# The last expert quad's down weights packed in rows of one expert, with one set of products behind the third unit

## The chip, the cores and the metric

One of the cores of a Trainium2 chip runs the kernel. The metric is the device time of one execution in microseconds.

## The reference

Two transformer blocks for 256 tokens of width 1024 (272 with the meta tokens in the first mixer), all in float32. The first block is a mixer (a gated linear recurrence and an RG-LRU branch), then a routed mixture of experts. The second has dilated attention, spatial gating and a dense feed-forward. The change touches the mixture of experts. There are 32 experts, in 4 groups of 8; each token takes 2 experts of one group. Each expert computes

```
y = (silu(xb @ w_gate[e]) * (xb @ w_up[e])) @ w_down[e]
y * wts
```

with w_gate and w_up of 1024 x 512 and w_down of 512 x 1024. The results are added to the tokens with their routing weights, and a norm follows, with which the second block begins.

## The kernel before

The kernel is written for the engines by hand: each engine has its own program, and they meet at semaphores. The 32 experts are done in 8 quads of 4 experts. Each expert has room for 32 tokens (CAP), so a quad fills 128 rows. TensorE works on the four experts of a quad in four column groups of 32, which run side by side.

**Units and slots.** The weights of a quad are 24 MB. SP loads them as 12 units of 2 MB (j = 0 to 11): four of w_gate, four of w_up, four of w_down. Units lie in 12 slots of SBUF, in an order given by MOE_SLOTS; unit m waits until `unit_used` tells that the unit 12 before it is used. In most quads a unit is the whole matrix of one expert (`whole(q, j)`), 16 KB in a row on each partition. In the last quad the down units (j = 8 to 11) are split otherwise. w_down is viewed as (p k) n: partition p holds four rows k = 0 to 3 of 1024 floats, 4 KB each, which lie behind one another in memory. Units 8, 9 and 10 hold row k = 0, 1 and 2 of all four experts (`expert_unit`, one transfer each, four pieces of 4 KB on each partition). Unit 11 holds row k = 3 of all four in two transfers, columns 0 to 511 and then 512 to 1023, in pieces of 2 KB (L642 and L643; the second counts on a semaphore of its own, `last_landed`). `load` (L580) issues a transfer and lets it add 16 to the semaphore `landed<slot>`; `landed_values` (line 137) works out the values that `take_moe` (L1249) waits for on TensorE. Behind the experts' units SP issues, in the same queue, the units of block 2: first five or more of w_in_2 (2 MB each, pieces of 2 KB), each when its slot is free.

**TensorE in a quad.** `products_of_four` (L1199) multiplies the tokens with the four gate units, then with the four up units. ScalarE and VectorE make the hidden values of them; `turn_hidden` (L1205) and `turn_weights` (L1211) turn them, and ScalarE copies them to `hT` (L1981). In quads 1 to 6 `down_of_four` (L1237) waits for the four down units and does 32 matmuls. In the last quad `down` (L1227) is called for k = 0, 1, 2: it waits for unit 8 + k, does 8 matmuls (2 halves of 512 columns x 4 experts) into banks 2 and 3, and gives the unit back with `unit_used`. In the trace a float32 matmul has two records, so 8 matmuls are x16.

**The end of the stage.** `down_last(0)` (L1245) waits for unit 11's first transfer and finishes columns 0 to 511. ScalarE copies bank 2 (L2021), `combine((0,))` (L1218) adds the result to the tokens (four matmuls of 128 x 512), `down_last(1)` does the other half once `last_landed` is there. VectorE copies the sums (L2773), `turn_half(0)` (L1341) turns them, `combine((1,))` follows. Then `take2(0)` waits for w_in_2's first unit, and `steps` (L1353) begins its products. The second half is copied and turned behind the first of them; the norm's statistics are applied later. From there on block 2 runs.

**Slots.** Units 8, 9, 10 of the last quad lie in slots 8, 1 and 2. Slots 1 and 2 are taken next by w_in_2's fifth and sixth unit (B2_SLOTS), which wait for `unit_used` of 94 and 95.

Of the kernel before, what the change touches and what calls it, by code (L numbers as in the profile page):

```python
# [25 lines left out]
CAP = 32  # L26
QE = P // CAP
# [30 lines left out]
MOE_UNITS = QUADS * QUNITS  # L58
# [4 lines left out]
NSLOT = 12  # L63
MOE_SLOTS = [11, 5, 3, 6, 7, 4, 0, 9, 8, 1, 2, 10]
# [21 lines left out]
def whole(q, j):  # L86

    return not (q == 0 and j < 8) and not (q == QUADS - 1 and j >= 8)


def transfers(name, block):

    return 2 if (name == "lru" or (block == 2 and name.startswith("ff"))) else 1


def b1_slot(u):

    return u % RING1
# [39 lines left out]
def landed_values():  # L138


    total = [0] * NSLOT
    b1, moe, b2 = [], [], []
    for u, name in enumerate(B1_UNITS):
        total[b1_slot(u)] += 16 * transfers(name, 1)
        b1.append(total[b1_slot(u)])
    for m in range(MOE_UNITS):
        total[MOE_SLOTS[m % NSLOT]] += 32 if m == NSLOT - 1 else 16
        moe.append(total[MOE_SLOTS[m % NSLOT]])
    for n, name in enumerate(B2_UNITS):
        total[B2_SLOTS[n % RING]] += 16 * transfers(name, 2)  # L150
        b2.append(total[B2_SLOTS[n % RING]])
    return b1, moe, b2


LANDED1, LANDED_MOE, LANDED2 = landed_values()


# [116 lines left out]
def build(nc, A, out):  # L274
    ctx = ExitStack()
    with ctx:
# [5 lines left out]
        def S(name):  # L282
            if name not in sems:
                sems[name] = ctx.enter_context(nc.semaphore(name))
            return sems[name]

        bank = [ctx.enter_context(nc.psum_tensor(f"bank{b}", [P, 512], F32)) for b in range(8)]
# [21 lines left out]
        def slot(k):  # L309

            if k == NSLOT - 1:
                return extra[:, :]
            return ring[:, k, :] if k < RING else arena[:, WORK + (k - RING) * UW:WORK + (k - RING + 1) * UW]

        def w3(s, k):
            return slot(s).rearrange("p (k n) -> p k n", k=k)
# [82 lines left out]
        def bufs(o, ysb, sg):  # L399
            return Bufs(o[:, 0:D].rearrange("p (c n) -> p c n", c=KC), o[:, D:D + DE].rearrange("p (k n) -> p k n", k=4),  # L400
                        o[:, 1536:1792].rearrange("p (t e s) -> p t e s", t=NT, e=QE),
                        o[:, 1792:2048].rearrange("p (t e s) -> p t e s", t=NT, e=QE),
                        o[:, 2048:2304].rearrange("p (t n) -> p t n", t=NT), ysb, sg)

        hrow = h.rearrange("p t d -> p (t d)")
        main = bufs(arena, hrow[:, 0:D], hrow[:, D:D + DE])
# [168 lines left out]
        def _(sp):  # L575
# [3 lines left out]
            def load(s, src, dst):  # L579
                sp.dma_start(dst, src).then_inc(S(f"landed{s}"), 16)  # L580
# [10 lines left out]
            for u, name in enumerate(B1_UNITS):  # L591
                s = b1_slot(u)
# [24 lines left out]
            down_w = A["w_down"][0].rearrange("e (p k) n -> p e k n", k=4)  # L617

            def expert_unit(j, e):
                j4 = j % 4  # L620
                if j < 8:
                    return (gate_w, up_w)[j // 4][:, bass.ds(e, QE), 2 * j4:2 * j4 + 2, :]
                return down_w[:, bass.ds(e, QE), j4:j4 + 1, :]

            def expert_dst(s, j):
                return slot(s).rearrange("p (e k n) -> p e k n", e=QE, k=2 if j < 8 else 1)
# [6 lines left out]
            def load_unit(s, q, j):  # L633

                if whole(q, j):
                    w = (gate_w, up_w, down_w)[j // 4][:, QE * q + j % 4, :, :]
                    load(s, w, slot(s).rearrange("p (k n) -> p k n", k=KC if j < 8 else 4))
                elif j < 11:
                    load(s, expert_unit(j, QE * q), expert_dst(s, j))
                else:  # L640
                    w = slot(s).rearrange("p (e n) -> p e n", e=QE)
                    load(s, down_w[:, QE * q:QE * q + QE, 3, 0:512], w[:, :, 0:512])  # L642
                    sp.dma_start(w[:, :, 512:1024], down_w[:, QE * q:QE * q + QE, 3, 512:1024]) \  # L643
                        .then_inc(S("last_landed"), 16)

            for m in range(MOE_UNITS):
# [16 lines left out]
                s = MOE_SLOTS[m % NSLOT]  # L663
# [21 lines left out]
                if m == NSLOT - 1:  # L685
                    load_last_down(slice(3, 4))
                else:
                    load_unit(s, m // QUNITS, m % QUNITS)


            for n, name in enumerate(B2_UNITS):
                s = B2_SLOTS[n % RING]
# [17 lines left out]
                else:  # L710
                    c = 4 * int(name[2:])
                    m = min(4, FC - c)
# [84 lines left out]
        def _(pe):  # L797
            mm = nc.tensor.matmul
            tr = nc.tensor.transpose

            def take1(u):
                pe.wait_ge(S(f"landed{b1_slot(u)}"), LANDED1[u])
                return b1_slot(u)
# [70 lines left out]
            for t in range(NT):  # L874
# [4 lines left out]
                for k in range(KC):  # L879
# [9 lines left out]
                    last = mm(b[:, :], rT[:, k, t * P:(t + 1) * P], w3(0, KC)[:, k, :], start=(k == 0), stop=(k == KC - 1))  # L889
# [171 lines left out]
            def columns(first, m):  # L1061

                return bank[first + m % 4][:, (m // 4) * T:(m // 4 + 1) * T]
# [6 lines left out]
            for m in (2, 6, 3, 7, 1, 5, 0, 4):  # L1070
# [4 lines left out]
                for k in range(HEADS):  # L1075
                    last = mm(columns(4, m), w3(b1_slot(13), 4)[:, k, m * P:(m + 1) * P],  # L1076
                              oT[:, k, :], start=(k == 0 and m < 4), stop=(k == HEADS - 1), skip_group_check=True)
            last.then_inc(S("projected_a"), 1)
            unit_out(pe, NH - 1)
            for part in range(2):  # L1080
                s = take1(14 + part)
                pe.wait_ge(S("ob_ready"), part + 1)
                for m in range(KC):
                    if part and m >= 4:
                        pe.wait_ge(S("merged"), m - 3)
                    for k in range(4):
                        last = mm(columns(0, m), w3(s, 4)[:, k, m * P:(m + 1) * P], ly[:, 4 * part + k, :],  # L1087
                                  start=(part == 0 and k == 0 and m < 4), stop=(part == 1 and k == 3),
                                  skip_group_check=True)
# [73 lines left out]
            def expert(s, n):  # L1163

                w = slot(s).rearrange("p (e n) -> p e n", e=QE)
                return w if n == 4 else w.rearrange("p e (k n) -> p e k n", k=2)
# [55 lines left out]
            def down(k, s, o=main):  # L1222

                w = expert(s, 4)
                for half in range(2):
                    for e in range(QE):
                        last = mm(bank[2 + half][e * CAP:(e + 1) * CAP, :], o.hT[:, k, e * CAP:(e + 1) * CAP],  # L1227
                                  w[:, e, half * 512:(half + 1) * 512], start=(k == 0), stop=(k == 3))
                return last

            def down_of_four(slots):
# [6 lines left out]
                                      w[e][:, k, half * 512:(half + 1) * 512], start=(k == 0), stop=(k == 3))  # L1238
                return last

            def down_last(half, s):

                w = expert(s, 4)
                for e in range(QE):
                    last = mm(bank[2 + half][e * CAP:(e + 1) * CAP, :], main.hT[:, 3, e * CAP:(e + 1) * CAP],  # L1245
                              w[:, e, half * 512:(half + 1) * 512], start=False, stop=True)
                return last

            def take_moe(m):  # L1249
                pe.wait_ge(S(f"landed{MOE_SLOTS[m % NSLOT]}"), LANDED_MOE[m])  # L1250
                return MOE_SLOTS[m % NSLOT]
# [34 lines left out]
            for q in range(QUADS):  # L1286
                m = QUNITS * q
# [36 lines left out]
                    pe.wait_ge(S("xgT_rest"), q + 2)  # L1324
                if q + 1 < QUADS:
                    down_of_four([take_moe(m + 8 + e) for e in range(QE)]).then_inc(S("unit_used"), QE)
            for k in range(3):
                down(k, take_moe(m + 8 + k)).then_inc(S("unit_used"), 1)
            down_last(0, take_moe(m + 11)).then_inc(S("first_half"), 1)
            pe.wait_ge(S("weights_copied"), QUADS)  # L1330
            pe.wait_ge(S("y_first"), 1)
# [125 lines left out]
            for p in range(PAIRS):  # L1457
# [15 lines left out]
                if p == 0:  # L1473
                    pe.wait_ge(S("s_diag"), 2)
                    for t in range(NT):
                        last = mm(bank[7][:, t * P:(t + 1) * P], ones[:, :], s_diag[:, t, :], start=True, stop=True)
# [12 lines left out]
                if p == PAIRS - 1:  # L1489
                    pe.wait_ge(S("ws_masked"), 1)  # L1490
                    pe.wait_ge(S("qk_copied"), 12)
                    for g in range(SG):
                        last = tr(bank[6 + g // 4][:, (g % 4) * P:(g % 4 + 1) * P], wsr[:, g * P:(g + 1) * P],
                                  ident[:, :])
# [8 lines left out]
            for n in range(AH):  # L1503
                j, tile = n // 2, n % 2
# [14 lines left out]
                for hh in range(2):  # L1519
                    for b in range(4):  # L1520
                        last = tr(bank[2 + hh][:, b * P:(b + 1) * P], sc[n % 2][:, hh, b * P:(b + 1) * P], ident[:, :])
# [10 lines left out]
                for b, (g, kt) in enumerate(blocks):  # L1532
                    for hh in range(2):
                        hd = 2 * j + hh
                        last = mm(bank[4 + 2 * (n % 2)][hh * HD:(hh + 1) * HD, 0:P],
                                  vv[:, kt, g * 512 + hd * HD:g * 512 + (hd + 1) * HD],
                                  PTb[:, hh * 512 + b * P:hh * 512 + (b + 1) * P], start=(b == 0), stop=(b == 3))
# [4 lines left out]
            for t in range(NT):  # L1542
                for g in range(SG):
                    last = mm(bank[4 + t][:, g * HD:(g + 1) * HD], wsT[:, g, :],
                              uv[:, t, 512 + g * HD:512 + (g + 1) * HD], start=True, stop=True)
# [13 lines left out]
            for q, (src, lo) in enumerate(((aT, 0), (sT, 4))):  # L1559
# [3 lines left out]
                for m in range(KC):  # L1563
# [4 lines left out]
                    for k in range(4):  # L1568
                        last = mm(columns(lo, m), w3(su, 4)[:, k, m * P:(m + 1) * P], src[:, k, :],  # L1569
                                  start=(k == 0), stop=(k == 3))  # L1570
# [119 lines left out]
            for n in range(FD_LAST):  # L1690
# [6 lines left out]
                for i in (5, 6, 7):  # L1697
                    last = down_product(i, n)
# [5 lines left out]
            for i in (1, 6, 5, 2, 3, 7, 4):  # L1704
                for n in range(FD_LAST, FD_UNITS):
                    last = down_product(i, n)
# [1575 lines left out]
```

## Time and profile before

| what | value |
|---|---|
| median of 3 runs | 1191.41 us (1190.79 to 1191.93) |
| profiled execution | 1192.67 us, its span 1190.6 us |
| TensorE (PE) busy | 1021.0 us, 86% |
| VectorE (DVE) busy | 532.7 us, 45% |
| ScalarE (ACT) busy | 220.4 us, 19% |
| moved by DMA | 318.51 MB, mean 268 GB/s |
| chain that ended last | PE 66%, DMA 29%, DVE 2% |
| mean granted clock of TensorE | 0.938 |

The span runs from the first to the last instruction in the profile; the execution's time is a little longer. The chain that ended last is followed back from the last instruction, at each step to what released it. TensorE's granted clock is given as a share of 2.4 GHz: 1.00 is 2.4 GHz, 0.50 is 1.2 GHz, and a stretch with both shows a mean. In rows of a timeline the idle time before an instruction and what ended it stand in square brackets. PE is TensorE, PEld its weight loads, SPq SP's queue with its DMA issues. "arena", "ring", "extra" and "bank" are memories: the slots lie in the first three, the banks are those of PSUM.

### The profile page before, as it was taken

The numbers are of one execution on the slowest core, as the hardware profiler recorded it, in microseconds if no ns is written. First come the engines' busy times: TensorE is split into PE (matmuls) and PEld (weight loads), VectorE is DVE, ScalarE is ACT, GpSimd is POOL, SyncE is SP. The second block draws the span as 40 slices with busy tenths as digits, with TensorE's granted clock in tenths as the row PEclk, the third lists the DMA queues.
The fourth block names the chain that finished last, engine by engine and source line by source line (L and its number), as shares of the span: only waits on it lengthen the run. The fifth ranks groups of instructions, "written<-read, shape, count | busy, mean of one in ns | idle before, by whom it ended". The sixth has DMA issues, their size and how long they took to land.

```text
span 1190.6 us, 15216 instructions
## 1 busy us (share of the span) xinstructions
PE 1021.0 (86%) x6492; PEld 680.7 (57%) x6492; DVE 532.7 (45%) x919; ACT 220.4 (19%) x459; POOL 17.1 (1%) x53
## 2 busy tenths in 40 slices
PE   8999999999747474747474689999999999999997
PEld 4999999855222222212222234444799859999743
DVE  6758847672110101000100038755887866566634
ACT  2535355011000000000000022222333101111001
POOL 1000000000000000000000010000000000000000
PEclk9999999999887887887887899999999999999999
DMA  9642438998999999999999995555442426644400
GB/s 343 208 159 82 138 139 303 347 353 364 429 429 428 427 426 428 429 426 428 428 428 427 415 389 217 185 194 197 167 143 74 140 86 216 193 161 157 163 0 35
DMA packets 88542, 318.51 MB, mean 268 GB/s; under 512 B 8852, under 2 KB 34568, under 8 KB 77720
## 3 DMA queue, kind: packets, MB, share of 16 engines
q1 hardware_dynamic: 80560, 314.58, 67.7%
q10 hardware_dynamic: 7912, 2.92, 1.0%
q8 instruction: 53, 0.87, 0.3%
q14 instruction: 17, 0.14, 0.0%
HBM read 316.44 MB, written 1.05 MB: 267 GB/s over the span
## 4 chain that ended last, share of the span: by engine, by line
PE 66%; DMA 29%; DVE 2%; SPq 1%; ACT 1%; issue 1%; POOL 0%; POOLq 0%; DVEq 0%; ACTq 0%
DMA arena<-in_w_up 27%; PE bank L910 11%; PE bank L1602 11%; PE bank L1453 9%; PE bank L1685 6%; PE bank L1199 5%; PE bank L1386 4%; PE bank L1113 4%; DMA ring<-in_w_in 3%; PE bank L1569 2%; PE bank L1087 2%; PE bank L1190 1%; PE bank L1076 1%; PE bank L889 1%; PE bank L985 1%; PE bank L1443 1%
## 5 line engine op out<-in xcount | busy, mean ns | idle before, releaser
L1199 PE MATMUL bank<-arena 128*32 128x512 f32 x336 | 124.5, 724 | 51.1 <-DMA arena<-in_w_up 51.1
L1199 PE MATMUL bank<-ring,arena 128*32 128x512 f32 x448 | 124.5, 719 | 0.0
L2735 DVE TENSOR_TENSOR h<-h,bank 128x512 f32<-128x512 f32 x8 | 5.5, 687 | 265.0 <-PE bank L1199 254.3
L1199 PE MATMUL bank<-extra,arena 128*32 128x512 f32 x112 | 60.4, 702 | 63.3 <-DMA arena<-in_w_gate 63.3
L1237 PE MATMUL bank<-arena 128*32 128x512 f32 x224 | 61.4, 709 | 37.2 <-DMA arena<-in_w_down 36.7
L1453 PE MATMUL bank<-ring,arena 128*128 128x512 f32 x200 | 87.1, 593 | 0.0
L1199 PEld LDWEIGHTS bank<-arena 128*32 128x32 f32 x336 | 31.4, 131 | 96.9 <-issue 96.9
L1602 PE MATMUL bank<-arena,ring 128*128 128x128 f32 x704 | 82.4, 275 | 0.0
L1602 PEld LDWEIGHTS bank<-arena,ring 128*128 128x128 f32 x704 | 80.5, 192 | 0.5 <-DVE arena L2235 0.2
L1199 PEld LDWEIGHTS bank<-extra,arena 128*32 128x32 f32 x112 | 13.7, 127 | 106.8 <-issue 106.8
L1453 PEld LDWEIGHTS bank<-ring,arena 128*128 128x128 f32 x200 | 37.6, 190 | 45.6 <-issue 45.4
L1237 PE MATMUL bank<-ring,arena 128*32 128x512 f32 x224 | 61.3, 710 | 0.0
L1237 PEld LDWEIGHTS bank<-arena 128*32 128x32 f32 x224 | 17.1, 128 | 76.7 <-issue 76.0
L910 PE MATMUL bank<-arena,ring 128*128 128x128 f32 (+1 forms) x400 | 49.4, 277 | 0.0
L910 PEld LDWEIGHTS bank<-arena,ring 128*128 128x128 f32 x400 | 47.4, 191 | 1.0 <-issue 0.8
L2832 DVE COPY h<-bank 128x512 f32<-128x512 f32 x7 | 4.8, 692 | 93.4 <-PE bank L1237 93.4
L1602 PE MATMUL bank<-arena 128*128 128x128 f32 x384 | 45.8, 275 | 0.0
L1602 PEld LDWEIGHTS bank<-arena 128*128 128x128 f32 x384 | 44.3, 192 | 0.0
L1685 PE MATMUL bank<-ring,arena 128*128 128x512 f32 x88 | 38.7, 592 | 0.0
L910 PE MATMUL bank<-ring 128*128 128x128 f32 (+1 forms) x304 | 36.8, 276 | 0.0
L910 PEld LDWEIGHTS bank<-ring 128*128 128x128 f32 x304 | 35.6, 192 | 0.2
L1113 PE MATMUL bank<-ring,arena 128*128 128x512 f32 x80 | 35.3, 592 | 0.0
(473 smaller groups left out, 1744.1 us busy)
## 6 DMA issues: line engine op xcount, KB each, us to landing
ring<-in_w_in SPq DMA_DIRECT2D x26, 2048.0 KB, 13.5
ring<-in_w_gate SPq DMA_DIRECT2D x16, 2048.0 KB, 39.9
arena<-in_w_up SPq DMA_DIRECT2D x16, 2048.0 KB, 35.0
ring<-in_w_up SPq DMA_DIRECT2D x16, 2048.0 KB, 39.5
ring<-in_w_down SPq DMA_DIRECT2D x16, 2048.0 KB, 39.9
arena<-in_w_down SPq DMA_DIRECT2D x14, 2048.0 KB, 35.5
extra<-in_w_gate SPq DMA_DIRECT2D x8, 2048.0 KB, 34.7
arena<-in_w_gate SPq DMA_DIRECT2D x8, 2048.0 KB, 48.0
```

The source lines that it names most:

```text
L889: last = mm(b[:, :], rT[:, k, t * P:(t + 1) * P], w3(0, KC)[:, k, :], start=(k == 0), stop=(k == KC - 1))
L910: last = mm(b[:, q * n:(q + 1) * n], lhs[:, k, q * P:(q + 1) * P], rhs[:, k, :], start=(start and q == 0 and k == 0), stop=(k == 3), skip_ ...
L985: last = mm(o, zc, zc, start=True, stop=True)
L1087: last = mm(columns(0, m), w3(s, 4)[:, k, m * P:(m + 1) * P], ly[:, 4 * part + k, :], start=(part == 0 and k == 0 and m < 4), stop=(part = ...
L1113: last = mm(bank[OUT_BANK[nth][i]][:, :], a[:, k, :], b[:, k, :], start=(k == 0), stop=(k == 3))
L1199: last = mm(bank[b][e * CAP:(e + 1) * CAP, :], main.xgT[:, k, e * CAP:(e + 1) * CAP], w[e][:, k, :], start=(k == 0), stop=(k == KC - 1))
L1237: last = mm(bank[2 + half][e * CAP:(e + 1) * CAP, :], main.hT[:, k, e * CAP:(e + 1) * CAP], w[e][:, k, half * 512:(half + 1) * 512], start ...
L1386: last = mm(o[:, q * P:(q + 1) * P], lhs[:, k, q * P:(q + 1) * P], rhs[:, k, :], start=(start and q == 0 and k == 0), stop=(k == 3), skip_ ...
L1453: last = mm(b[:, :], lhs[:, k, :], rhs[:, k, :], start=(start and k == 0), stop=(k == 3), skip_group_check=True)
L1569: last = mm(columns(lo, m), w3(su, 4)[:, k, m * P:(m + 1) * P], src[:, k, :], start=(k == 0), stop=(k == 3))
L1602: last = mm(b[:, q * P:(q + 1) * P], lhs(q, k), rhs(k), start=(start and q == 0 and k == 0), stop=(k == 3), skip_group_check=True)
L1685: last = mm(bank[SUM_BANK[i]][:, :], lhs, rhs, start=(f == 0), stop=(f == FU - 1), skip_group_check=True)
```

## The change

Units 8, 9 and 10 of the last quad each hold the three rows k = 0, 1, 2 of one expert (experts 0, 1, 2 of the quad) and behind them one row of the fourth: k = 0 in unit 8, 1 in unit 9, 2 in unit 10. Each comes in two transfers, one with 12 KB in a row on each partition and one with 4 KB, and its landing value is 32 higher in place of 16. `down_packed` takes the place of the three calls of `down`: it waits for all three units, does the same 24 matmuls in the same order (k, half, expert), with the rows taken from where they lie now, and adds 3 to `unit_used` at its end. Unit 11 stays as it is. SP's order of the units stays too.

```diff
     for m in range(MOE_UNITS):
-        total[MOE_SLOTS[m % NSLOT]] += 32 if m == NSLOT - 1 else 16
+        total[MOE_SLOTS[m % NSLOT]] += 32 if m == NSLOT - 1 or MOE_UNITS - 4 <= m < MOE_UNITS - 1 else 16
         moe.append(total[MOE_SLOTS[m % NSLOT]])
...
                     load(s, w, slot(s).rearrange("p (k n) -> p k n", k=KC if j < 8 else 4))
+                elif j < 8:
+                    load(s, expert_unit(j, QE * q), expert_dst(s, j))
                 elif j < 11:
-                    load(s, expert_unit(j, QE * q), expert_dst(s, j))
+                    load(s, down_w[:, QE * q + j - 8, 0:3, :], w3(s, 4)[:, 0:3, :])
+                    load(s, down_w[:, QE * q + 3, j - 8:j - 7, :], w3(s, 4)[:, 3:4, :])
...
+            def down_packed(slots):
+
+                w = [w3(s, 4) for s in slots]
+                for k in range(3):
+                    for half in range(2):
+                        for e in range(QE):
+                            row = w[e][:, k, :] if e < 3 else w[k][:, 3, :]
+                            last = mm(bank[2 + half][e * CAP:(e + 1) * CAP, :], main.hT[:, k, e * CAP:(e + 1) * CAP],
+                                      row[:, half * 512:(half + 1) * 512], start=(k == 0), stop=False)
+                return last
+
...
-            for k in range(3):
-                down(k, take_moe(m + 8 + k)).then_inc(S("unit_used"), 1)
+            down_packed([take_moe(m + 8 + k) for k in range(3)]).then_inc(S("unit_used"), 3)
             down_last(0, take_moe(m + 11)).then_inc(S("first_half"), 1)
```

## Rows read from the trace of the kernel before

**Rows 1.** Chain of waits, 620 to 760 us: start us, us, what.
```profile
625.67 49.19 DMA arena<-in_w_up
...
681.90 20.59 DMA ring<-in_w_in
...
728.36 1.09 PE bank L1377 x8
```

**Rows 2.** Stretches: busy time by engine, then TensorE's clock, DMA share, GB/s.
```profile
540.00:560.00 20.00, 13.29 (x80) 4.24 (x76) 0.00 (x0) 1.06 (x1) 0.00 (x0) 0.84 1.01 427
...
674.00:684.00 10.00, 8.34 (x64) 2.36 (x64) 0.53 (x1) 0.00 (x0) 0.00 (x0) 0.82 1.02 406
...
690.00:702.50 12.50, 8.75 (x48) 2.92 (x48) 3.87 (x6) 1.93 (x3) 0.00 (x0) 1.00 1.05 386
```

**Rows 3.** TensorE's timeline: start us, us, line, operation, count, idle before and its cause.
```profile
684.70 0.38 PE L1211 MATMUL bank<-ident,arena 128*128 128x128 f32 x2
...
685.55 1.92 PE L1227 MATMUL bank<-arena 128*32 128x512 f32 x16 [0.47 <-ACT arena L1981]
...
687.29 1.90 PE L1227 MATMUL bank<-ring,arena 128*32 128x512 f32 x16
...
690.27 1.92 PE L1227 MATMUL bank<-ring,arena 128*32 128x512 f32 x16 [1.07 <-DMA ring<-in_w_down]
...
692.98 1.06 PE L1245 MATMUL bank<-arena 128*32 128x512 f32 x8 [0.79 <-DMA arena<-in_w_down]
...
694.85 1.96 PE L1218 MATMUL bank<-h,arena 128*128 128x512 f32 x4 [0.81 <-ACT h L2021]
...
698.19 1.09 PE L1341 MATMUL bank<-ident,h 128*128 128x128 f32 x8 [0.39 <-DVE h L2773]
...
699.12 1.88 PE L1218 MATMUL bank<-h,arena 128*128 128x512 f32 x4
...
702.53 1.98 PE L1353 MATMUL bank<-ring,arena 128*128 128x512 f32 x4 [1.52 <-DMA ring<-in_w_in]
```

**Rows 4.** SP's issues in order of time; time to landing of L643.
```profile
668.73 0.51 SPq L580 DMA_DIRECT2D arena<-in_w_down  x1
...
669.28 12.57 SPq L643 DMA_DIRECT2D arena<-in_w_down  x1
...
DMA to landing us min/median/max: 26.4/26.4/26.4
...
704.17 5.29 SPq L580 DMA_DIRECT2D ring<-in_w_in  x1
```

**Rows 5.** L1237, the down products of the quads before: waits; one of them.
```profile
  DMA arena<-in_w_down: 36.7, 6
...
398.18 1.03 PE L1237 MATMUL bank<-arena 128*32 128x512 f32 x1 [5.43 <-DMA arena<-in_w_down]
```

**Rows 6.** Stretches of six down groups (L1237) and of 690.3: busy, clock.
```profile
339.40:346.90 7.50, 7.50 (x56) 2.31 (x60) 0.75 1.00 426
398.20:405.00 6.80, 6.80 (x52) 2.10 (x56) 0.79 1.02 434
456.90:466.00 9.10, 9.10 (x60) 2.60 (x64) 0.69 1.00 427
517.10:525.00 7.90, 7.90 (x60) 2.44 (x64) 0.78 1.01 429
575.80:583.00 7.20, 7.20 (x56) 2.20 (x60) 0.80 1.01 430
634.50:643.70 9.20, 9.18 (x61) 2.66 (x64) 0.70 1.01 426
...
690.30:692.30 2.00, 1.89 (x16) 1.00 1.06 390
```

**Rows 7.** Stretches of two of the gaps before them, columns as in rows 2.
```profile
392.80:398.10 5.30, 0.00 (x0) 0.00 (x0) 0.74 (x3) 0.36 (x1) 0.00 (x0) 0.96 0.98 417
509.60:517.00 7.40, 0.00 (x0) 0.00 (x0) 0.72 (x3) 0.34 (x1) 0.00 (x0) 0.78 1.01 427
```

## The prediction, made before the changed kernel ran

> **What bounds the kernel now.** I read the chain of waits first. In the expert stage it consists of one long transfer of expert weights a quad: the last, 49.19 us, ends at 674.86, then come the products on the last quad's up weights, and then, from 681.90, 20.59 us of a transfer of w_in, until TensorE goes on at 702.5 [rows 1]. From there the chain runs through TensorE and a stretch of VectorE and is back on TensorE at 728.36 [rows 1] and stays there, with short breaks. So the expert stage is bound by DMA, and what follows by work that starts with the matmuls of L1353 at 702.53. A change inside the last quad counts by how much it moves that start, and that shift then goes into the end unchanged.
>
> Two things must be there for that start: w_in's first unit, and TensorE, which has to finish the end of the expert stage first. The table of stretches shows the DMA engines full the whole time: 427 GB/s with whole units (16 KB rows), 406 GB/s in the stretch of the last quad's 4 KB rows, 386 GB/s in the 2 KB rows of the last unit and of w_in [rows 2]. The timeline of TensorE shows the other side [rows 3]: three down groups (L1227) start at 685.55, 687.29 and 690.27, the last after an idle 1.07 us for its weights; the first half of the last unit at 692.98; then a chain of copy, combine, copy, turn, combine, whose last group starts at 699.12; then 1.52 us idle until 702.53.
>
> **What the change does to the transfers.** The same 6 MB come in the same place of SP's queue, as six issues instead of three, with rows of 12 KB and 4 KB in place of four of 4 KB. From the rates a 2 MB unit takes 2.097/0.427 = 4.91 us with 16 KB rows and 2.097/0.406 = 5.17 with 4 KB rows. The difference of 0.26 us is the price of three more rows per partition; the change takes two of them away, 0.17 us a unit, 0.5 us for three. Bounds: 0 (rows nobody joins) and 3 x 0.26 = 0.8 us (as good as 16 KB rows). I take 0.5, since the two rates bracket the new form on both sides.
> The Trainium skill, "DMA: Bandwidth & Descriptors" (its table of figures at the top), says that a transfer reaches line rate from 512 bytes up. By that rule the rows gain nothing and the sum below would be 0.5 us worse; the three rates of [rows 2] speak against it.
> Three more issues on SP cost it some 0.5 us each (0.51 for the one at 668.73 [rows 4]), but SP is far ahead: w_in's first unit is issued at 681.90 and lands 20.6 us later [rows 1], and the issue before it is itself held up for 12.57 us by what is queued [rows 4]. A unit that comes as two transfers costs no extra: the first half of the last one ended TensorE's wait at 692.98 [rows 3], the second, issued at 669.28, landed 26.4 us later, at 695.7 [rows 4], and 2.7 us are 1.049 MB at 388 GB/s, the plain rate. I take 0. If SP weren't ahead it would be 1.5 us.
> The slots of the three units are now given back together, after all their products, at about 696 instead of 687 to 692. The transfers of block 2 that need them are w_in's fifth and sixth; the fifth was issued at 704.17 [rows 4], so 8 us of cover remain: 0.
>
> **What it does to TensorE.** Now 24 matmuls begin when the last of three units is there: at 690.27 - 0.5 = 689.8. They are as many as before. One group of eight takes 687.29 - 685.55 = 1.74 us [rows 3], three take 5.2, so down_last's first half starts at 695.0 instead of 692.98, 2.0 us later. Two of three groups used to run while the third unit was in flight; that cover is gone. The first half of the last unit has long landed by then, so its wait of 0.79 disappears, which is in this sum.
> From 692.98 to 699.12 each step waits for the one before (ScalarE's copy 0.81 us, VectorE's copies 0.39 us) [rows 3], none for a transfer; so the whole chain moves by the 2.0 us. Combine's last group of four takes 4 x 0.43 = 1.7 us: TensorE could have started L1353 at 700.8, 1.7 us before it did (the idle of 1.52 us goes by modelled ends and is the lower bound). With w_in there at 702.0, the start moves by 2.0 - 1.7 = **+0.3 us**, between 0 and +1.0 by the bounds so far.
>
> **The clock.** TensorE is now without matmuls from the end of the turns, 685.1, to 689.8: 4.7 us. Before, it had 0.47 and 1.07 us there [rows 3]. What such a gap costs is shown by the six quads between: their down products each wait for a transfer, 36.7 us in six waits, one of 5.43 us among them [rows 5]. All six start at the lower clock, 1.2 GHz: with the mean granted clock c over a group of length t, the time lost is (1-c) x t: in order 0.25 x 7.5 = 1.9, then 1.4, 2.8, 1.7, 1.4 and 2.8 us [rows 6]. In the gap of 5.3 us that ended at 398.1 the mean clock was 0.96, in that of 7.4 us it was 0.78 [rows 7]; so the fall came in the last 0.4 us of the one, and 3.3 us before the end of the other. At 690.27, after 1.07 us, the clock was still 1.00 [rows 6]. A gap of 4.7 us is shorter than the waits of [rows 5 to 7], but much nearer to them than to 1.07. So I expect the lower clock, with a loss as in the four shorter cases, 1.4 to 1.9; I take 1.75. Bounds: 0, and 5.2 if all 12 steps of 0.43 us run at half clock.
> The Trainium skill, "TensorE: Matmul & The Clock Gate" (HAM oscillation), says that short bursts of matmuls with waits on DMA between them start again at the half clock each time. By it alone the case below without a fall would have no chance; the 1.07 us gap shows that the length matters.
>
> **Sum.** +2.0 late, -1.7 slack, +1.75 clock = +2.05 us. The profiled execution took 1192.67 us (span 1190.6), 1.26 over the median of 1191.41; I put the shift on the median: **1193.4 us**. That is +0.17%. About 0.2%, 2.4 us, is what a measurement of this kernel can tell from no change.
>
> **The rivals.**
> - The clock falls and stays low for over 4.2 us, as in two of the six cases: loss 2.8, shift 0.3 + 2.8 = +3.1: 1194.5, slower. Its place is the packed groups, its price half of the time at 1.2 GHz, and it decides from a loss of 2.1 us up. Against it only that four of six were shorter. 0.27.
> - The clock doesn't fall: shift +0.3, 1191.7, no change. For it: the gap is shorter than any of the six. 0.18.
> - The transfers gain the full 0.8 us and the clock holds. Then the packed groups start at 689.5, TensorE is ready at 702.5, and w_in is there at 701.7: 1191.4. The gain is eaten by TensorE. For a start 1 us earlier than before the transfers would have to gain 1.8 us, over twice the bound. 0.04.
> - The change doesn't do what it says for the transfers: the three rows move as single ones, gain 0. With the expected clock +2.55: 1194.0. 0.06.
>
> **Chances.** The forecast 0.45, the rivals as above. Slower by over 0.2%, above 1193.8, are the case of the long fall and that of the unjoined rows: 0.33 together. Faster by over 0.2% would need what no row shows; I give it 0.03, out of the case without a fall. The rest, 0.64, is within 0.2%. The range of 8 in 10: down to 1191.3, which takes in most of the case without a fall, up to 1195.0, which takes in the long fall with some noise.
>
> **What the profile would show.** Right: the first of the packed matmuls at about 689.8 after an idle time of some 4.7 us, put down to a transfer of down weights; a granted clock of 0.5 there and first steps of 0.85 us instead of 0.43; the last unit's products with no wait; L1353 at about 704.5, with no wait for w_in, or almost none. Wrong: landings at the same times as before (no gain), a clock of 1.00 through the gap, or w_in still what L1353 waits for. If the third unit landed over 1.5 us earlier, the sum fails at the transfers.

## The result and the profile after

| | median | runs |
|---|---|---|
| before | 1191.57 us (1190.72 to 1192.62) | 11 |
| changed | 1193.77 us (1193.34 to 1195.31) | 11 |

The ratio is 1.0021, with a 95% interval of 1.0013 to 1.0030: 2.2 us slower, +0.18% by the medians. The interval excludes 1, so this is a change, if a small one. The profiled execution took 1193.75 us, its span is 1191.8 us; that of before took 1192.67. In the runs below, single executions of 1760 and 4956 us of before and one of 1364 us of the probe with two idle matmuls are slow ones and are left out of the ratios.

The chain of waits of the changed kernel, start, us, what, answers to [rows 1]. The transfer of w_in has left it. In its place stands the transfer of the third down unit, until 689.4, and then, from 689.51, a chain of work only.

```profile
654.12 35.26 DMA ring<-in_w_down
689.51 6.67 PE bank L1251 x48
696.18 0.90 PE bank L1259 x8
697.10 0.61 ACT h L2034
697.85 1.97 PE bank L1221 x4
...
703.99 1.72 PE bank L1366 x4
```

TensorE's timeline answers to [rows 3]:

```profile
684.96 0.38 PE L1214 MATMUL bank<-ident,arena 128*128 128x128 f32 x2
689.51 1.03 PE L1251 MATMUL bank<-arena 128*32 128x512 f32 x1 [4.17 <-DMA ring<-in_w_down]
...
692.07 0.67 PE L1251 MATMUL bank<-ring,arena 128*32 128x512 f32 x2
...
692.58 0.60 PE L1251 MATMUL bank<-ring,arena 128*32 128x512 f32 x3
...
696.00 1.04 PE L1259 MATMUL bank<-arena 128*32 128x512 f32 x8
...
703.83 1.88 PE L1366 MATMUL bank<-ring,arena 128*128 128x512 f32 x4
```

The packed products (L1251) start at 689.51, 4.17 us after the turns, put down to a down unit's transfer. A step is one of the two records of a float32 matmul; the four column groups take theirs side by side. Three steps of 0.85 us lead from there to 692.07, from 692.58 on a step takes 0.43. The last unit's products (L1259) start at 696.00 without a wait, three microseconds later than the 692.98 of before. L1366 (L1353 before) follows at 703.83 with no idle time.

The stretches, columns as in [rows 2]: the clock falls near the end of the gap, is 0.80 in the mean over the packed products, and the last unit's transfers and w_in still move at 387 GB/s.

```profile
685.20:690.00 4.80, 0.63 (x6) 0.23 (x8) 0.42 (x1) 0.55 (x1) 0.00 (x0) 0.88 1.01 387
689.00:697.00 8.00, 7.49 (x56) 2.10 (x56) 0.00 (x0) 0.00 (x0) 0.00 (x0) 0.80 1.05 386
690.00:702.50 12.50, 11.31 (x77) 3.83 (x70) 1.91 (x4) 1.20 (x2) 0.00 (x0) 0.91 1.05 387
```

SP's issues answer to [rows 4]. SP is even further ahead than before: w_in's first unit is issued at 676.23 and lands 24.0 us later, at 700.2.

```profile
662.68 13.50 SPq L646 DMA_DIRECT2D arena<-in_w_down  x1
676.23 38.15 SPq L580 DMA_DIRECT2D ring<-in_w_in  x6
```

To compare executions, times below are also given from the start of the last quad's first up product, since that point itself differs by over 1 us between profiles (674.99 and 673.79 in two profiles of before, 674.54 in that of the changed kernel). From there to L1353 it was 27.54 us before and 29.29 after. By the same measure w_in's first unit landed 27.5 us in before and 25.7 after, 1.8 us earlier; but TensorE came to L1366 only 3.6 us after that landing, so it bought nothing. Where the 1.8 us come from is taken up at the end of the experiments.

### The profile page after: what moved, and what is told of

Same layout as the page of the kernel before. It is cut to its first block, busy times and chain, and to the rows that moved or that the text cites. A ratio compares the mean times of both kernels' runs of the same rounds, so it can differ in the third digit from the quotient of the medians.

```text
span 1191.8 us, 15220 instructions
## 1 busy us (share of the span) xinstructions
PE 1026.3 (86%) x6492; PEld 682.7 (57%) x6492; DVE 532.6 (45%) x919; ACT 220.6 (19%) x459; POOL 17.1 (1%) x53
## 4 chain that ended last, share of the span: by engine, by line
PE 68%; DMA 26%; DVE 2%; SPq 2%; ACT 1%; issue 1%; POOL 0%; POOLq 0%; DVEq 0%; ACTq 0%
DMA arena<-in_w_down 23%; PE bank L913 11%; PE bank L1615 11%; PE bank L1466 9%; PE bank L1698 6%; PE bank L1240 5%; PE bank L1399 4%; PE bank L1116 4%; DMA ring<-in_w_down 3%; PE bank L1582 2%; PE bank L1090 2%; SPq L580 2%; PE bank L892 1%; PE bank L1193 1%; PE bank L1079 1%; PE bank L988 1%
## 5 line engine op out<-in xcount | busy, mean ns | idle before, releaser
L1202 PE MATMUL bank<-arena 128*32 128x512 f32 x336 | 126.9, 731 | 48.7 <-DMA arena<-in_w_up 48.7
L1202 PE MATMUL bank<-ring,arena 128*32 128x512 f32 x448 | 126.9, 731 | 0.0
L1202 PE MATMUL bank<-extra,arena 128*32 128x512 f32 x112 | 63.0, 727 | 62.4 <-DMA arena<-in_w_gate 62.4
L1240 PE MATMUL bank<-arena 128*32 128x512 f32 x224 | 62.2, 717 | 38.0 <-DMA arena<-in_w_down 37.6
L1240 PE MATMUL bank<-ring,arena 128*32 128x512 f32 x224 | 62.1, 718 | 0.0
```

The costliest lines, as they stand in the source:

```text
L1202: last = mm(bank[b][e * CAP:(e + 1) * CAP, :], main.xgT[:, k, e * CAP:(e + 1) * CAP], w[e][:, k, :], start=(k == 0), stop=(k == KC - 1))
```

## Experiments

All ratios against before are from runs on the same chip, with 95% intervals; 0.0010 is 1.2 us. The experiments ran on three chips, on which before had medians of 1191.15, 1191.43 and 1191.51 us. So two experiments are compared by what each is over its own before, or by position, if they weren't on one chip. Eleven runs each, where nothing else is said.

**The gap filled.** Does the clock cost anything, or the late start alone?

```diff
+            busy(0, 4)
             down_packed([take_moe(m + 8 + k) for k in range(3)]).then_inc(S("unit_used"), 3)
```

> The changed kernel with four idle-time matmuls (128 x 512, 3.4 us) put between the turns and the packed products, their result unused. My theory: the change loses 2.0 us by starting 24 matmuls late, 1.3 to 1.8 us by the clock's fall in the 4.2 us gap, and gets 1.7 us of slack back. With the gap filled the clock stays at 1.00, the packed products take 5.15 us instead of 6.49, the last unit's products start at 694.7 instead of 696.0, and the time is 0 to 0.4 us over the kernel before (1.3 to 2 us under the changed one). Rival A, the clock costs nothing that counts and the late start is all: as the changed kernel, 2.2 us over before. Rival B, the transfers or their issues cost the time: as the changed kernel too, and the landing of w_in's first unit would end the wait at L1353.

Measured: 1192.47 us, ratio 1.0012 (1.0003 to 1.0021), 1.3 us over before. TensorE's timeline, and the stretch of the packed products:

```profile
685.68 3.70 PE L1143 MATMUL bank<-h,ident 128*128 128x512 f32 x8 [0.47 <-ACT arena L1995]
689.80 0.59 PE L1251 MATMUL bank<-arena 128*32 128x512 f32 x1 [0.43 <-DMA ring<-in_w_down]
...
694.95 1.07 PE L1259 MATMUL bank<-arena 128*32 128x512 f32 x8
696.82 1.95 PE L1221 MATMUL bank<-h,arena 128*128 128x512 f32 x4 [0.80 <-ACT h L2035]
...
702.80 1.88 PE L1367 MATMUL bank<-ring,arena 128*128 128x512 f32 x4
```

```profile
689.40:695.00 5.60, 5.20 (x52) 1.96 (x56) 0.00 (x0) 0.00 (x0) 0.00 (x0) 1.00 1.05 387
```

The clock stays at 1.00, the packed products take 694.95 - 689.80 = 5.15 us instead of 6.49, and L1353's counterpart starts at 702.80, 27.9 us after the first up product instead of 29.3. So the clock is part of the loss, 1.1 us by the ratios and 1.4 by position. By the ratios alone rival A would still be possible, since the intervals of this kernel and of the changed one overlap; the profile speaks against it, and two kernels timed on one chip settle it (below, half the filler). Rival B doesn't fit either: the filler touches no transfer, and no wait for w_in appears. But 1.3 us over before was more than the 0 to 0.4 I had said. In the first profile of before L1353 starts at 27.54, which would make 0.4. The interval, 0.4 to 2.5 us, doesn't quite exclude that; it pointed at the baseline.

**The wait alone,** with the transfers of before:

```diff
-            for k in range(3):
-                down(k, take_moe(m + 8 + k)).then_inc(S("unit_used"), 1)
+            s3 = [take_moe(m + 8 + k) for k in range(3)]
+            for k in range(3):
+                last = down(k, s3[k])
+            last.then_inc(S("unit_used"), 3)
```

> The kernel before, its transfers untouched, but the three down groups start only when all three units are there. My theory: start at 690.3, low clock, last unit's products at about 697, L1353 at about 704.8: 2.5 to 3.3 us over before, which is 0.3 to 0.8 us more than the changed kernel, as the gain of the packed transfers is missing. Rival B (the cost of the change lies in its transfers): no change against before. Rival A: 0.8 us over before.

Measured: 1194.94 us (5 runs, 1193.91 to 1196.56), ratio 1.0035 (1.0022 to 1.0049).

```profile
689.24 3.61 PE L1227 MATMUL bank<-arena 128*32 128x512 f32 x16 [3.98 <-DMA ring<-in_w_down]
...
696.08 1.06 PE L1245 MATMUL bank<-arena 128*32 128x512 f32 x8
...
703.93 1.88 PE L1355 MATMUL bank<-ring,arena 128*128 128x512 f32 x4
```

The cost is there without any change to the transfers: 3.8 us over before by the medians. Rivals A and B are out. Start to last unit is 696.08 - 689.24 = 6.84 us, a clock loss of 1.7. L1355 starts 703.93 - 673.91 = 30.02 us after the first up product, 0.7 us later than in the changed kernel's profile. Its runs spread over 2.65 us; that the clock loss differs from one to the other, as it did from quad to quad in [rows 6], fits this, but only one of them has a profile.

**The wait alone with the gap filled,** the fourth corner of wait and clock:

```diff
+            busy(0, 4)
             s3 = [take_moe(m + 8 + k) for k in range(3)]
```

> The transfers of before, products only when all three units are there (as in the kernel with the wait alone, which came out 3.8 us over before), with the four idle matmuls of 3.4 us in the gap. My theory: the clock stays up, which gives back 1.3 to 1.8 us as it did with packed transfers (1.3 us there): 2.0 to 2.5 us over before. The difference to the packed transfers with filler is then the gain of the transfers, 0.5 to 1.2 us. Rival A, the clock counts for nothing: 3.8 us over before.

Measured: 1192.81 us, ratio 1.0010 (1.0001 to 1.0019).

```profile
684.83 3.70 PE L1140 MATMUL bank<-h,ident 128*128 128x512 f32 x8 [0.47 <-ACT arena L1984]
689.41 1.92 PE L1227 MATMUL bank<-arena 128*32 128x512 f32 x16 [0.88 <-DMA ring<-in_w_down]
...
694.55 1.07 PE L1245 MATMUL bank<-arena 128*32 128x512 f32 x8
...
702.41 1.88 PE L1356 MATMUL bank<-ring,arena 128*128 128x512 f32 x4
```

The 24 matmuls take 5.14 us here too, 1.7 us less than without the filler, and L1356 starts 28.3 us after the first up product instead of 30.0. By the medians, each over its own before, the filler gives back 3.8 - 1.4 = 2.4 us with these transfers. The time is 1.4 us over before, where I had said 2.0 to 2.5. The filler with packed transfers was 1.3 us over its before, so the times don't tell the two forms of transfer apart. The positions do: the products start 689.41 - 674.08 = 15.33 us after the first up product, there 689.80 - 674.90 = 14.90, and L1353's counterpart comes at 28.3 against 27.9. The packed transfers gain 0.4 us, less than my 0.5 to 1.2 for this run.

**Two units first, then one,** with the changed kernel's transfers: experts 0, 1 and the fourth's two rows when units 8 and 9 are there.

```diff
-            down_packed([take_moe(m + 8 + k) for k in range(3)]).then_inc(S("unit_used"), 3)
+            w = [w3(take_moe(m + 8 + u), 4) for u in range(2)]
+            for k in range(3):
+                for half in range(2):
+                    for e in (0, 1, 3) if k < 2 else (0, 1):
...
+            last.then_inc(S("unit_used"), 2)
+            w2 = w3(take_moe(m + 10), 4)
+            for k in range(3):
+                for half in range(2):
...
+            last.then_inc(S("unit_used"), 1)
```

> The changed kernel's transfers, but experts 0 and 1 (and the fourth's two rows) are done as soon as units 8 and 9 are there, and only expert 2 and one row of the fourth after unit 10. My theory: no clock fall, but a column group works through its own 12 steps of 0.43 us in a row, whoever stands beside it. So 12 steps remain after unit 10, and the first part, from 685.8, runs until 690.9: last unit's products at about 696.1, L1353 at 703.9, 1.2 to 1.6 us over before. Rival C, that waiting for all three units is what costs and two thirds of the work can be taken out of the way: 8 of 24 matmuls are left, 1.7 us, last unit's products at 692, at or under the kernel before.

Measured: 1192.40 us, ratio 1.0010 (1.0001 to 1.0019).

```profile
689.01 0.62 PE L1352 MATMUL bank<-ring,arena 128*32 128x512 f32 x1
...
692.48 0.62 PE L1259 MATMUL bank<-arena 128*32 128x512 f32 x2
...
693.75 0.59 PE L1352 MATMUL bank<-ring,arena 128*32 128x512 f32 x1
...
696.00 1.95 PE L1221 MATMUL bank<-h,arena 128*128 128x512 f32 x4 [0.80 <-ACT h L2050]
...
701.99 1.88 PE L1382 MATMUL bank<-ring,arena 128*128 128x512 f32 x4
```

The size came as expected, 1.2 us, not every position: L1382 starts at 701.99, where I had said 703.9. Expert 2's products (L1352) begin at 689.01, 0.5 us after unit 10 landed, beside those of the first two, and the first groups of the last unit's products (L1259) overtake them at 692.48. What holds is that expert 2's column group works through its 12 steps in a row: the last begins at 693.75, 4.74 us or 11 steps of 0.43 after the first. The whole gains nothing on the kernel with the filler: combine starts 696.00 - 673.70 = 22.3 us after the first up product, there 696.82 - 674.90 = 21.9, and the medians on the same chip are 1192.40 and 1192.47 us. Rival C is out: with a unit per expert, what follows the last landing is a full 12 steps of one column group, although only 8 of 24 matmuls are left. Before, it was 4 steps.

**Pairs.** Units 8 and 9 with rows 0 and 1 of two experts each, in 8 KB pieces, and unit 10 as before:

```diff
+                elif j in (8, 9):
+                    e = QE * q + 2 * (j - 8)
+                    load(s, down_w[:, e:e + 2, 0:2, :], slot(s).rearrange("p (e k n) -> p e k n", e=2, k=2))
                 elif j < 11:
...
-            for k in range(3):
-                down(k, take_moe(m + 8 + k)).then_inc(S("unit_used"), 1)
+            w = [slot(take_moe(m + 8 + u)).rearrange("p (e k n) -> p e k n", e=2, k=2) for u in range(2)]
+            for k in range(2):
+                for half in range(2):
+                    for e in range(QE):
...
+            last.then_inc(S("unit_used"), 2)
+            down(2, take_moe(m + 10)).then_inc(S("unit_used"), 1)
```

> The kernel before with units 8 and 9 holding rows 0 and 1 of two experts each (8 KB pieces), unit 10 as before; the products of rows 0 and 1 start when 8 and 9 are there, those of row 2 when 10 is. My theory: both units have landed at 685, so nothing is late and the clock stays up; the pieces save two thirds of 0.26 us in two units, 0.35 us: 0.3 to 0.5 us under before, too little to be told. Rival D: packed rows bring w_in's first unit earlier than the plain rates say (in the changed kernel it landed at 700.2 instead of 702.5), then L1353 can start when TensorE is ready, at 700.5 to 701: 1.5 to 2 us under before.

Measured: 1190.84 us, against a median of 1191.15 us for before on that chip; ratio 1.0001 (0.9992 to 1.0010): no difference that can be told.

```profile
688.84 1.92 PE L1230 MATMUL bank<-ring,arena 128*32 128x512 f32 x16 [0.67 <-DMA ring<-in_w_down]
691.56 1.06 PE L1248 MATMUL bank<-arena 128*32 128x512 f32 x8 [0.79 <-DMA arena<-in_w_down]
...
700.72 1.98 PE L1362 MATMUL bank<-ring,arena 128*128 128x512 f32 x4 [1.14 <-DMA ring<-in_w_in]
```

The products of row 2 keep their place behind unit 10, 14.97 us after the first up product (before 15.28), the clock stays up. L1353's counterpart still waits for w_in, 1.14 us. So this form takes the pieces' gain without the wait, and its gain is too small to see. Rival D's 1.5 us didn't come.

**How large is the slack?** The kernel before once more, and twice with idle matmuls that delay TensorE alone, behind the last combine:

```diff
             combine((1,)).then_inc(S("combined"), 1)
+            busy(2, 2)
```

> The kernel before, once more under the profiler. Theory S: the slack of 1.7 us read from the first profile was that of one late landing. There w_in's first unit landed 6.8 us behind the last unit's second half; in four other profiles, one of them with the transfers of before, it was 5.4 to 6.5. Then L1353 starts 26 to 27 us after the first of the last quad's up products (27.5 in the first profile) with less wait than 1.5 us, and the profiled time lies at 1191 to 1192. Rival T: the first profile is typical: 27.5 us and a wait of about 1.5 us again.

> The kernel before with two idle matmuls (128 x 512, together 1.7 us of TensorE) behind the last combine, ahead of the wait for w_in's first unit, their result unused. It delays TensorE by 1.7 us there and nothing else. Rival T, slack 1.5 to 1.7 us in every execution: 0 to 0.2 us over before. Theory S, a typical slack of 0.2 to 0.8 us: 0.9 to 1.5 us over before.

> As the probe with two, with four idle matmuls, 3.4 us. Rival T: 1.7 to 1.9 us over before. Theory S: 2.6 to 3.2 us over before. The difference of the two probes should be 1.7 us under both, if the delay goes into the end unchanged once the slack is gone, as the prediction assumed.

Measured: before again 1190.79 us in its profile, a median of 1191.21 us in 8 runs, ratio 1.0000 (0.9990 to 1.0010); two idle matmuls 1191.85 us, ratio 1.0005 (0.9996 to 1.0015), +0.6 us; four 1193.60 us, 1.0019 (1.0010 to 1.0028), +2.3 us. The timelines of before again and of the four:

```profile
691.74 1.07 PE L1245 MATMUL bank<-arena 128*32 128x512 f32 x8 [0.78 <-DMA arena<-in_w_down]
...
697.88 1.88 PE L1218 MATMUL bank<-h,arena 128*128 128x512 f32 x4
700.76 1.98 PE L1353 MATMUL bank<-ring,arena 128*128 128x512 f32 x4 [0.99 <-DMA ring<-in_w_in]
```

```profile
700.66 3.60 PE L1140 MATMUL bank<-h,ident 128*128 128x512 f32 x8
704.10 1.88 PE L1354 MATMUL bank<-ring,arena 128*128 128x512 f32 x4
```

The slack is the time from TensorE's being ready for L1353 to w_in's landing. Two delays of 1.72 and 3.44 us cost 0.6 and 2.3, which gives a slack of 1.1 to 1.2 us; their difference of 1.7 goes into the end in full. These times alone don't exclude 1.7 us, since each has an interval of some 1 us to either side. The profiles are sharper. In the second of before combine's last group ends at 697.88 + 1.72 = 699.60, L1353 starts at 700.76, 1.16 us later and 26.97 us after the first up product. In the two probes w_in's first unit landed 1.0 us (701.13 against 698.41 + 1.72) and 1.2 us (701.83 against 698.94 + 1.72) after that group's end. In the first profile it was 1.7 us and 27.54. So neither T (1.5 to 1.7) nor S (0.2 to 0.8) was right: three of four profiles have a slack of 1.0 to 1.2 us. The first was of an execution 1.1 us slower than the median, and 0.5 us of that is its later landing of w_in.

**The changed kernel again:**

> The changed kernel once more under the profiler. My account: the packed products start 4.2 to 4.7 us after the turns, at the lower clock, and need 1.3 to 2.9 us more than the 5.15 us of full clock, the loss depending on the execution; L1353 starts with no wait for w_in, 29 to 31 us after the first of the last quad's up products (29.3 in the first profile).

Measured: 1193.93 us median of 8 runs, ratio 1.0019 (1.0009 to 1.0029).

```profile
689.00 0.94 PE L1251 MATMUL bank<-arena 128*32 128x512 f32 x1 [3.75 <-DMA ring<-in_w_down]
...
695.84 1.07 PE L1259 MATMUL bank<-arena 128*32 128x512 f32 x8
...
703.70 1.88 PE L1366 MATMUL bank<-ring,arena 128*128 128x512 f32 x4
```

The packed products take 695.84 - 689.00 = 6.84 us, a clock loss of 1.7, and L1366 starts 703.70 - 674.06 = 29.6 us after the first up product. Why 1.7 us here and 1.3 in the first profile can be seen in the stretch before the products, in the first profile and in this one:

```profile
685.20:689.00 3.80, 0.14 (x2) 0.00 (x0) 0.42 (x1) 0.55 (x1) 0.00 (x0) 0.97 1.01 388
```

```profile
685.20:689.00 3.80, 0.05 (x1) 0.03 (x1) 0.42 (x1) 0.46 (x1) 0.00 (x0) 1.00 1.01 389
```

In the first the clock had already fallen when the gap ended, so part of the slow time cost nothing; here it was still 1.00 at 689.00, and the whole of the slow time lies in the products.

**Half the filler:**

```diff
-            busy(0, 4)
+            busy(0, 2)
```

> The changed kernel with two idle matmuls (1.7 us) instead of four in the gap; they come first, so some 2.3 us without matmuls remain ahead of the packed products. If only a gap near 4 us or more brings the clock down, it stays at 1.00 and the time is as with the full filler, 1.1 to 1.5 us over before. If any gap of over 2 us does, it is as the changed kernel, 2.0 to 2.5 us over before.

Measured: 1192.33 us, ratio 1.0008 (0.9999 to 1.0017), as with the full filler. On the same chip the changed kernel had 1193.93 us: 1.6 us more, and only one of the eleven runs here (1194.12 us) lies in the range of its eight (1193.27 to 1195.30). Rival A of the first experiment is out by this.

```profile
686.67 1.98 PE L1143 MATMUL bank<-h,ident 128*128 128x512 f32 x4 [0.47 <-ACT arena L1995]
689.49 0.59 PE L1251 MATMUL bank<-arena 128*32 128x512 f32 x1 [0.83 <-DMA ring<-in_w_down]
...
694.63 1.07 PE L1259 MATMUL bank<-arena 128*32 128x512 f32 x8
```

The clock stayed at 1.00. But the turns came late in this execution, so only 1.1 us without matmuls were left (686.67 + 1.72 = 688.39 to 689.49). Two idle matmuls suffice. No run here has a gap between 1.1 and 3.75 us, so what such a gap would do to the clock stays open, and with it the question that this run was to answer.

**Why w_in's first unit lands late.** In the first profile of before it landed 6.8 us behind the last unit's second half, in the changed kernel's 700.2 - 694.8 = 5.4. Near these landings there is a transfer of 16 KB on the instruction queue. In before it starts between the two, in the changed kernel behind both. The rows (packets, MB, share of the 16 engines) are of before, 698.0 to 699.2, and of the changed kernel, 701.0 to 702.2:

```profile
q8 instruction: 1, 0.02, 5.5%
```

```profile
q8 instruction: 1, 0.02, 5.5%
```

It starts 0.3 us behind the start of the turns of the first half in both, at 698.5 and 701.5, so it moves with TensorE's place in its program. In two kernels 228 waits that are long fulfilled were added to TensorE's program, to move it:

```diff
+                if 0 < q < QUADS - 1:
+                    for _ in range(38):
+                        pe.wait_ge(S("hT_ready"), q + 1)
                 if q + 1 < QUADS:
                     down_of_four([take_moe(m + 8 + e) for e in range(QE)]).then_inc(S("unit_used"), QE)
```

> The kernel before with 38 waits on a semaphore that has long been reached, in front of the down products of each of quads 1 to 6, 228 in all, where TensorE waits for transfers anyway. They do nothing but lengthen its program. Theory F: in the profiles a 16 KB transfer of the instruction queue runs 0.3 us behind the start of the turns of the first half (698.5 in the first profile of before, 701.5 in that of the changed kernel); where it runs ahead of the landing of w_in's first unit, that landing comes 6.2 to 6.8 us behind the last unit's second half, in the others 5.4. The added instructions shift the block boundary to some 28 instructions later, behind the wait of L1353. Then the unit lands 5.4 us behind, and L1353 starts about 26.1 us after the first up product instead of 27: 0.7 to 1.0 us under before. Rival G, the landing is late for another reason: 6.2 us or more as before, no change in time.

> The kernel with units 8 and 9 in pairs (0.3 us under before) with the same 228 waits. Theory F: w_in's first unit lands 5.4 us behind the last unit's second half, L1353 starts about 25.8 us after the first up product: 1.2 to 1.5 us under before, the fastest of all. Rival G: 0.3 us under before.

Measured: before with the waits 1191.87 us, ratio 1.0009 (1.0000 to 1.0018); pairs with the waits 1191.17 us, 0.9993 (0.9983 to 1.0002). The first one's instruction queue from 689.5 to 690.7, its timeline, and that of the pairs:

```profile
q8 instruction: 1, 0.02, 5.5%
```

```profile
692.62 1.07 PE L1245 MATMUL bank<-arena 128*32 128x512 f32 x8 [1.49 <-DMA arena<-in_w_down]
...
700.75 1.98 PE L1356 MATMUL bank<-ring,arena 128*128 128x512 f32 x4
```

```profile
693.66 1.07 PE L1248 MATMUL bank<-arena 128*32 128x512 f32 x8 [2.01 <-DMA arena<-in_w_down]
...
701.78 1.98 PE L1365 MATMUL bank<-ring,arena 128*128 128x512 f32 x4
```

The transfer moved, but to 689.6 and 690.3, ahead of its old place and not behind it. And with it the late landing moved: w_in's first unit lands 5.4 us behind the last unit's second half in both (700.7 after 695.3, and 701.8 after 696.4), while the last unit's first half now lands 3.4 and 4.2 us behind unit 10 where it was 2.7. TensorE's wait for it grew from 0.79 to 1.49 and 2.01 us. So in these two kernels and in the profiles of before the late landing, by 0.7 to 1.5 us, is the one next after this transfer. Rival G is out: the late landing of w_in went when the transfer went. What makes one transfer cost 0.7 us and another 1.5 stays open. Nothing was won: the delay sits ahead of the whole chain instead of ahead of w_in. L1353's counterparts start 26.8 and 27.3 us after the first up product, where I had said 26.1 and 25.8. The 0.7 to 1.0 us hoped for with before and the 1.2 to 1.5 with the pairs didn't come, and none of the kernels tried is faster than before beyond its interval.

How far this goes is shown by the other landings. From 300 to 630 us the units have rows of 16 KB and land 4.9 us apart. In all fourteen profiles together, of 627 landings with no such instruction transfer since the landing before last, none comes over 0.2 us late. Of 156 spaces between landings with one in it, 36 are followed by a late landing, that one or the next. So no landing there was late without an instruction transfer, but three in four of these transfers delay nothing. In the last quad too: in before one starts at 678.65, and the unit it runs in lands 5.12 us after the one ahead of it, as do the two that follow without one; with the full filler one starts at 700.48, just ahead of w_in's first landing at 700.52, and that landing and the next come after 5.4 us each. What decides whether a transfer delays one is not shown.

## Why the prediction was right

The forecast was 1193.4 us, +2.05 us as three terms (1191.41 + 2.05 is 1193.46); the result is +2.2 us at 1193.77. The forecast change lies within the measured interval of +1.5 to +3.6 us, and the positions that were named in the timeline came within 1 us, but for w_in's landing. The mechanism was right: late start, lower clock, less the slack. That the sum came so near is in part luck, as the last term shows.

- **The late start, +2.0 us.** With the clock held up (filler) the last unit's products start 694.95 - 674.90 = 20.05 us after the first up product, in before again 691.74 - 673.79 = 17.95: 2.1 us. The 24 matmuls took 5.15 us at full clock against 5.2 said.
- **The transfers, 0.5 us in it.** TensorE's products for which the third unit was awaited start 14.97, 14.94 and 14.90 us after the first up product with packed transfers and 15.28, 15.33 and 15.33 without: 0.4 us, within the bounds of 0 and 0.8. The rivals of unjoined rows and of the full 0.8 us both fall with it. The Trainium skill's figure in "DMA: Bandwidth & Descriptors" (Specifications), line rate from 512 bytes up, gives 0; these traces disagree with it by the 0.4 us, and by 427 GB/s with rows of 16 KB against 387 with rows of 2 KB. What the sum missed is w_in: put at 702.0, it landed at 700.2. By the distance from the first up product that is 1.8 us earlier than in the first profile of before, 0.4 us by the packed rows and 1.4 as no instruction transfer ran ahead of it. It cost the forecast nothing, since TensorE was the later of the two by 3.6 us.
- **The clock, +1.75 us.** 6.49 - 5.15 = 1.3 us in the first profile and 1.7 in the second; by the medians 1.6 us on one chip (1193.93 against 1192.33 with half the filler). The gap was 4.17 us instead of 4.7, as the turns came a little later. The case without a fall did not occur in the three profiles with such a gap (4.17, 3.75 and 3.98 us). The Trainium skill, "TensorE: Matmul & The Clock Gate" (HAM oscillation), says that matmuls after a wait on DMA start at the half clock again; all three profiles agree, with first steps of 0.8 to 0.86 us instead of 0.43. The rival of the long fall, a loss of 2.8 us, occurred in none of the three profiles; whether it did in single runs of 1195.3 us is not shown.
- **The slack, -1.7 us.** This is the term that was mis-sized: 1.0 to 1.2 us by the second profile and the probes. It was read from one execution whose w_in landed later than usual. The prediction had noted that this execution was 1.26 us over the median, but took nothing from that. Late start 2.1, clock 1.3 to 1.7 and slack -1.0 to -1.2 make 2.2 to 2.8, where 2.2 was measured and 2.4 in the second set of runs. The slack had taken off 0.5 to 0.7 us too much, the clock term put on up to 0.45 too much: the two partly cancelled, and that is luck.
- **Into the end unchanged.** From L1353's start to the span's end it is 488.1 us in the first profile of before (1190.6 - 702.53), 488.1 in the second, 488.0 in the changed kernel's (1191.8 - 703.83), and 488.0 with four idle matmuls (1192.1 - 704.10).
- **SP and the slots.** That six issues cost nothing held: w_in's first unit was issued 5.7 us earlier than before (676.23 against 681.90). That the slots come free later cost nothing visible either, as the chain after L1366 is as long as before.

## What to carry to other kernels

A unit of weights that helps the DMA queue may harm the engine behind it: what counts is how much work remains after the last landing, per column group, and here it rose from 4 steps to 12. Where several units must be complete before work begins, the wait can also lower TensorE's clock, as it did here after 3.75 to 4.17 us; two idle matmuls in the gap took that part back, and cost nothing that was measured. And a slack on the critical path should be read from several profiles: one gave 1.7 us here, three others 1.0 to 1.2. Probes with a known delay agreed, but their times alone, with intervals of 1 us to either side, would not have told the two apart.

## What the runs showed that was not expected

An instruction transfer of 16 KB, between weights that fill the DMA engines, can make a landing late, here by 0.7 to 1.5 us. Its place follows TensorE's place in its program, so a change in the number of instructions far ahead moves it: 228 added waits took the delay from w_in's first unit (6.8 us in the first profile of before and 6.3 in the second, down to 5.4) to the last unit's first half (2.7 us up to 3.4 and 4.2). Most such transfers delay nothing, 120 of 156 between 300 and 630 us; what sets the others apart is open. Which engine's program it carries was inferred from its position alone.
